# First projection of two dense MLP layers as seven block products, with pairs of column chunks and a joined ReLU and square

## The reference, cut to what matters

```python
def sq_relu_mlp(h, w1, w2):
    return jnp.square(jax.nn.relu(h @ w1)) @ w2
# h: 256 tokens x 1024,  w1: 1024 x 4096,  w2: 4096 x 1024   (twice: after S5, after attention)
```

## Time and profile before

| | |
|---|---|
| median of three timed runs | 1896.58 us |
| the profiled execution | 1891.4 us |
| its span, first to last instruction | 1889.4 us |
| TensorE busy | 1585.1 us, 84% |
| VectorE busy | 635.8 us, 34% |
| ScalarE busy | 231.5 us, 12% |
| mean granted TensorE clock | 0.924 |

### The profile page before, as it was taken

How to read it: one execution, slowest core, us unless ns; L and a number is a source line. 1 busy time by engine, 2 the same in 40 slices (tenths; PEclk the granted TensorE clock), 3 DMA queues, 4 the chain that set the end, 5 groups by cost and what they waited for, 6 DMA issues and landing times. The chain is left out here.

```text
span 1889.4 us, 28141 instructions
## 1 busy us (share of the span) xinstructions
PE 1585.1 (84%) x12561; PEld 1011.5 (54%) x12561; DVE 635.8 (34%) x1409; ACT 231.5 (12%) x519; POOL 75.3 (4%) x95
## 2 busy tenths in 40 slices
PE   8999768778776999966575756699999999999998
PEld 6654434444433885533232323488688446578743
DVE  5752233432233224212411111360213463421356
ACT  2311011001100000200200000120011002311000
POOL 2000100000000100000000000060000001000000
PEclk9999889888988999987888878799999999999999
DMA  9457999999998846899999999933534444234420
GB/s 334 151 225 285 383 425 425 425 425 423 424 425 347 322 185 279 348 420 424 412 407 426 421 426 422 382 147 132 192 140 152 153 138 159 90 134 148 164 89 22
DMA packets 88070, 540.03 MB, mean 286 GB/s; under 512 B 7342, under 2 KB 9454, under 8 KB 54156
## 3 DMA queue, kind: packets, MB, share of 16 engines
q1 hardware_dynamic: 86060, 531.24, 70.1%
q0 software_dynamic: 1888, 6.95, 1.0%
HBM read 531.89 MB, written 6.29 MB: 285 GB/s over the span
## 5 line engine op out<-in xcount | busy, mean ns | idle before, releaser
L759 PE MATMUL ps<-ring,work 128*32 128x256 f32 x3968 | 296.7, 460 | 224.4 <-DMA ring<-in_moe_w_up 222.7
L759 PEld LDWEIGHTS ps<-ring,work 128*32 128x32 f32 x3968 | 156.3, 127 | 352.6 <-issue 297.1
L710 PE MATMUL ps<-hT,ring 128*128 128x256 f32 (+2 forms) x1424 | 312.6, 382 | 0.0
L710 PEld LDWEIGHTS ps<-hT,ring 128*128 128x128 f32 x1424 | 269.8, 190 | 41.9 <-issue 2.5
L2115 DVE TENSOR_TENSOR rowb<-rowb,ps 128x128 f32<-128x128 f32 x64 | 18.3, 287 | 383.0 <-ACT rowb L1544 383.0
L772 PE MATMUL ps<-ring,multi 128*32 128x256 f32 x1984 | 122.5, 388 | 12.5 <-ACT multi L1549 12.5
L2121 DVE COPY multi<-ps 128x256 f32<-128x256 f32 x64 | 27.1, 424 | 264.4 <-PE ps L772 264.4
L1251 PE MATMUL ps<-ring,work 128*128 128x512 f32 x256 | 114.4, 592 | 0.0
L736 PE MATMUL ps<-ring,work 128*128 128x512 f32 x256 | 110.9, 593 | 0.0
L772 PEld LDWEIGHTS ps<-ring,multi 128*32 128x32 f32 x1984 | 58.9, 111 | 74.4 <-issue 23.7
L1251 PE MATMUL ps<-work 128*128 128x512 f32 x192 | 87.0, 592 | 0.0
(11 more groups left out here) (481 smaller groups left out, 1562.1 us busy)
## 6 DMA issues: line engine op xcount, KB each, us to landing
ring<-in_moe_w_gate SPq DMA_DIRECT2D x62, 2048.0 KB, 18.8
ring<-in_moe_w_up SPq DMA_DIRECT2D x62, 2048.0 KB, 23.4
ring<-in_moe_w_down SPq DMA_DIRECT2D x62, 2048.0 KB, 22.5
ring<-in_w_ff SPq DMA_DIRECT2D x32, 2048.0 KB, 8.3
ring<-in_sc_w_in SPq DMA_DIRECT2D x6, 2048.0 KB, 17.9
ring<-in_ssm_w_glu SPq DMA_DIRECT2D x4, 2048.0 KB, 19.1
ring<-in_lru_w_in SPq DMA_DIRECT2D x3, 2048.0 KB, 14.2
ring<-in_lru_w_out SPq DMA_DIRECT2D x2, 2048.0 KB, 23.5
```

The costliest lines, as they stand in the source:

```text
L710: mm = pe.matmul(ps[:, bank, 0:n], w[:, k, P * c:P * c + P], hT[:, k, t0:t0 + n], start=(k == 0), stop=(k == DC - 1))
L759: mm = pe.matmul(ps[32 * q:32 * q + 32, bank, 0:256].rearrange("p (u n) -> p u n", u=2), x[:, k, :], gu[:, k, :, 2 * P * (q // 2):2 * P * ...
```

## The change

Tokens and contraction are cut in two, and so are the two column chunks of a pair: with A the tokens (two blocks of 128 by two halves of the contraction of 512) and B the weights (two halves by two chunks of 128), seven products of sums of blocks replace eight products of blocks. A product is four accumulating matmuls of 128x128 by 128. VectorE makes three sums of weight blocks and one in place for each piece of w1 (`first_weights`), four sums of token blocks once a layer (`first_tokens`), and joins the seven products of each pair (`join`) after ScalarE copied one of them out of PSUM. The last instruction of the join takes the ReLU and the square in one. A pair takes two PSUM banks, and four pairs are in flight. The weight sums of pieces 0 and 1 are made before `mix_norm`. The attention's `oT` moves to another region.

```diff
-        for kind in ("ff_proj", "ff_relu", "ff_sq"):
-            share(kind, [(f"{kind}{l}", DFF // P) for l in range(2)])
+        for kind in ("ff_pair", "ff_copied", "ff_sq"):
+            share(kind, [(f"{kind}{l}", NPAIR) for l in range(2)])
...
-                add(f"ff1_{layer}_{j}", cols(a["w_ff1_2"][layer], 512 * j, 512), (f"ff_proj{layer}", 4 * j + 4))
+                add(f"ff1_{layer}_{j}", cols(a["w_ff1_2"][layer], 512 * j, 512), (f"ff_pair{layer}", 2 * j + 2))
...
+        pair_bank = ((2, 6), (3, 7), (4, 0), (5, 1))
+        def pair_part(j, first, n=1):
+            bank, at = next((pair_bank[j % 4][i], row.index(first)) for i, row in enumerate(((2, 6, 1, 3), (4, 5, 7))) if first in row)
+            return ps[:, bank, P * at:P * at + P * n]
...
+        def first_factors(layer, j, i):
+            p_, q = j // 2, j % 2
+            t1, t2, t4 = (t[:, :, q, :] for t in first_sums(p_))
+            b11, t3, b21, b22 = (piece_of(layer, p_, k1, e)[:, :, q, :] for k1 in range(2) for e in range(2))
+            return {1: (b11, hT_b[0][:, 0:4]), 2: (b21, hT_b[0][:, 4:8]), 3: (b22, ff_s4), 4: (t4, hT_b[1][:, 4:8]),
+                    5: (t1, ff_s1), 6: (t2, ff_s2), 7: (t3, ff_s3)}[i]
...
-        oT = region(7424, HEADS, SEQ)
+        oT = region(8192, HEADS, SEQ)
...
+            def pair_product(layer, j, i):
+                w, x = first_factors(layer, j, i)
+                for k in range(4):
+                    mm = pe.matmul(pair_part(j, i), w[:, k, :], x[:, k, :], start=(k == 0), stop=(k == 3), skip_group_check=True)
+                return mm
             def ff_first(layer, before_):
+                transposes(before_, [1, 2], f"{before_}_normed", only=0)
+                pe.wait_ge(*nth(f"{before_}_hT", 2))
+                for j in range(4):
+                    slot_wait(pe, f"ff1_{layer}_{j // 2}")
+                    for i in (1, 2):
+                        pair_product(layer, j, i)
+                transposes(before_, [1, 2], f"{before_}_normed", only=1)
+                pe.wait_ge(*nth(f"{before_}_hT", 4))
+                for j in range(4):
+                    pe.wait_ge(*nth(f"ff_weights{layer}", j // 2 + 1))
+                    pair_product(layer, j, 4)
+                pe.wait_ge(*nth(f"ff_tokens{layer}", 1))
+                for j in range(4):
+                    for i in (6, 5, 7, 3):
+                        mm = pair_product(layer, j, i)
+                    mm.then_inc(S(f"ff_pair{layer}"), 1)
+                for j in range(4, NPAIR):
+                    slot_wait(pe, f"ff1_{layer}_{j // 2}")
+                    pe.wait_ge(*nth(f"ff_sq{layer}", j - 3))
+                    for i in (1, 2):
+                        pair_product(layer, j, i)
+                    pe.wait_ge(*nth(f"ff_weights{layer}", j // 2 + 1))
+                    for i in (6, 5, 7, 4, 3):
+                        mm = pair_product(layer, j, i)
+                    mm.then_inc(S(f"ff_pair{layer}"), 1)
...
-                    pe.wait_ge(*nth(f"ff_sq{layer}", 4 * j + 4))
+                    pe.wait_ge(*nth(f"ff_sq{layer}", NPAIR - 1 if j == 0 else NPAIR))
...
-                    A(ff[:, c, :], ps[:, ff_bank(c), 0:SEQ], ACT.Relu).then_inc(S(f"ff_relu{layer}"), 1)
+                for j in range(NPAIR):
+                    act.wait_ge(*nth(f"ff_pair{layer}", j + 1))
+                    if j >= 4:
+                        act.wait_ge(*nth(f"ff_sq{layer}", j - 3))
+                    A(ff_p1[j % 4], pair_part(j, 1), ACT.Copy).then_inc(S(f"ff_copied{layer}"), 1)
...
+            def first_weights(layer, p_):
+                b11, b12, b21, b22 = (piece_of(layer, p_, k1, e) for k1 in range(2) for e in range(2))
+                t1, t2, t4 = first_sums(p_)
+                slot_wait(dve, f"ff1_{layer}_{p_}")
+                if p_ >= 4:
+                    dve.wait_ge(*nth(f"ff_pair{layer}", 2 * p_ - 2))
+                link(V.tensor_tensor(t1, b12, b11, ALU.subtract))
+                V.tensor_tensor(b12, b22, b12, ALU.subtract)
+                link(V.tensor_tensor(t2, b22, t1, ALU.subtract))
+                V.tensor_tensor(t4, b21, t2, ALU.subtract).then_inc(S(f"ff_weights{layer}"), 1)
+            def first_tokens(layer, before_):
+                a11, a12, a22 = hT_b[0][:, 0:4], hT_b[0][:, 4:8], hT_b[1][:, 4:8]
+                dve.wait_ge(*nth(f"{before_}_hT", 4))
+                link(V.tensor_tensor(ff_s1, ff_s3, a22, ALU.add))
+                V.tensor_tensor(ff_s3, a11, ff_s3, ALU.subtract)
+                link(V.tensor_tensor(ff_s2, ff_s1, a11, ALU.subtract))
+                V.tensor_tensor(ff_s4, a12, ff_s2, ALU.subtract).then_inc(S(f"ff_tokens{layer}"), 1)
+            def join(layer, j):
+                two_ = lambda t: t.rearrange("p (a n) -> p a n", a=2)
+                one = lambda t: t.unsqueeze(1).to_broadcast([P, 2, P])
+                even, odd, u = ff[:, 2 * j, :], ff[:, 2 * j + 1, :], two_(ff_u)
+                dve.wait_ge(*nth(f"ff_copied{layer}", j + 1))
+                link(V.tensor_tensor(two_(even), one(ff_p1[j % 4]), two_(pair_part(j, 2, 2)), ALU.add))
+                link(V.tensor_tensor(u, one(even[:, P:2 * P]), two_(pair_part(j, 5, 2)), ALU.add))
+                V.tensor_tensor(odd[:, 0:P], u[:, 0], pair_part(j, 3), ALU.add)
+                link(V.tensor_tensor(ff[:, 2 * j:2 * j + 2, P:2 * P], one(u[:, 1]), two_(pair_part(j, 4, 2)), ALU.add))
+                both = ff[:, 2 * j:2 * j + 2, :]
+                V.scalar_tensor_tensor(out=both, in0=both, scalar=0.0, in1=both, op0=ALU.max, op1=ALU.mult).then_inc(S(f"ff_sq{layer}"), 1)
+            def mlp(layer, before_):
+                first_tokens(layer, before_)
+                first_weights(layer, 2)
+                for j in range(NPAIR):
+                    join(layer, j)
+                    if j == 1:
+                        first_weights(layer, 3)
+                    elif j % 2 and 5 <= j < 12:
+                        first_weights(layer, (j + 3) // 2)
+                    elif j in (13, 15):
+                        piece_sums(layer, (j - 13) // 2)
...
+            for p_ in range(2):
+                first_weights(0, p_)
             mix_norm("s5")
...
+            for p_ in range(2):
+                first_weights(1, p_)
             mix_norm("mla")
```

More of the change, by code:

```diff
@@ L62 @@
 DFF = 4 * D
+NPAIR = DFF // P // 2
 BIG = 1.0e30
@@ L115, in first_and_second_block @@
         share("masked", [(f"masked{l}", 3 - l) for l in range(2)])
-        for kind in ("ff_proj", "ff_relu", "ff_sq"):
-            share(kind, [(f"{kind}{l}", DFF // P) for l in range(2)])
+        for kind in ("ff_pair", "ff_copied", "ff_sq"):
+            share(kind, [(f"{kind}{l}", NPAIR) for l in range(2)])
+        share("ff_weights", [(f"ff_weights{l}", 8) for l in range(2)])
+        share("ff_tokens", [(f"ff_tokens{l}", 1) for l in range(2)])
         share("dve_constants", [("par_ready", 1), ("lam", 1), ("soft", 1), ("p_half", 1), ("p_theta", 1), ("s5_coef", 1),
@@ L316, in region, with piece_of, first_sums @@
             return v
-        def ff_bank(c):
-            return 2 + c % 4 if c < DFF // P - 4 else (1, 6, 7, 5)[c % 4]
+        pair_bank = ((2, 6), (3, 7), (4, 0), (5, 1))
+        def pair_part(j, first, n=1):
+            bank, at = next((pair_bank[j % 4][i], row.index(first)) for i, row in enumerate(((2, 6, 1, 3), (4, 5, 7))) if first in row)
+            return ps[:, bank, P * at:P * at + P * n]
+        def piece_of(layer, p_, k1, e):
+            w = slot_view(f"ff1_{layer}_{p_}", DC, 512).rearrange("p k (q e n) -> p k q e n", q=2, e=2)
+            return w[:, 4 * k1:4 * k1 + 4, :, e, :]
+        def first_sums(p_):
+            at = (2048, 5120)[p_] if p_ < 2 else 8192 + 4096 * (p_ % 2)
+            return [region(at + 1024 * i, 4, 2, P) for i in range(3)]
+        hT_b = [hT[:, :, NMETA + P * b:NMETA + P * b + P] for b in range(2)]
+        ff_s1, ff_s2, ff_s4 = (t.rearrange("p (k n) -> p k n", k=4) for t in (rowb[:, 0:512], rowb[:, 512:1024], tmp_a[:, 0:512]))
+        ff_s3 = hT_b[1][:, 0:4]
+        ff_p1 = [tmp_a[:, 512 + P * i:512 + P * i + P] for i in range(4)]
+        ff_u = multi[:, 2048:2048 + 2 * P]
+        def first_factors(layer, j, i):
[4 more added lines that the diff above has]
+                    5: (t1, ff_s1), 6: (t2, ff_s2), 7: (t3, ff_s3)}[i]
         product_bank = {1: 2, 2: 0, 3: 1, 4: 7, 5: 4, 6: 3, 7: 6}
@@ L1233, in _ @@
             rows_out("s5", [1, 2], ["s5_out0", "s5_out1"], s5_y, NMETA, "glu_done")
-            def ff_first(layer, before_):
[L1237 to L1245, removed]
+            def pair_product(layer, j, i):
[3 more added lines that the diff above has]
+                return mm
+            def ff_first(layer, before_):
+                transposes(before_, [1, 2], f"{before_}_normed", only=0)
[23 more added lines that the diff above has]
+                    mm.then_inc(S(f"ff_pair{layer}"), 1)
             def product(layer, i, j):
@@ L1266, in ff_second @@
```

(20 more changed lines are left out.)

## The result

The changed kernel took 1870.26 us (median of four runs, 1868.70 to 1873.58) against 1894.44 us before (four runs, 1890.48 to 1896.86): ratio 0.9875, 95% interval 0.9858 to 0.9892. The forecast was 1873 us in a range of 1865 to 1884. The profiled execution took 1868.7 us, with a span of 1866.9; the sum had given 1869.6.

What follows compares the result with a forecast made beforehand. TensorE's matmul instruction count times spacing was taken to bound both first projections; saving 21.8 us from 1891.4 gave 1869.6 by the profiled execution, 1874.8 on the median's scale. Forecast 1873 us, range 1865 to 1884.

Steps and rivals of the forecast that it cites:

- The distance of matmuls: First projections: matmul instructions 128 columns wide follow each other every 0.1117 us, 256 wide every 0.2158; upper bound 0.1153.
- TensorE, term by term: First projections, after the second token block is ready: 103.85 us becomes 92.93 for 832 instructions, saving 10.9 us a layer.
- VectorE's new work: Beside the first projections: join 2.3 us, weight sums 4.9, token sums 2.8; VectorE keeps up with 3 us to spare.
- The due times: When TensorE wants each VectorE result in the first projections: no stall booked, up to 1 us a layer allowed.
- The hand-over: Start of the second projection: join 14 waits behind w2's 6.13 us piece sums, ready 91.5, wanted 92.9, cover 1.4 us.
- Due time (1): Token sums at the first projection's start: ready 2.8 us, wanted 3.57; at contended speed 4.1, 0.5 us late.
- Ahead of the norm: Before the MLP norm: the first two weight sums, 9.8 us, fit VectorE's idle 12.90 and 13.31 us.
- Sum: Whole kernel: 1891.4 less 21.8 gives 1869.6 us by the profiled execution, 1874.8 on the median's scale; 1873 given.
- A: First projections: contended VectorE becomes the bound, join 3.45 us; with undisturbed sums from about 4.4; 1907 us, chance 0.05.
- B: Only the hand-over stalls: joins of 3.5 to 4.0 us make join 14 late; 1875 to 1884 us, chance 0.09.
- C: First projections: each 128-wide instruction waits for its own 192 ns weight load; 2004 us, chance 0.01.
- D: First projections: spacing is 0.1153 us and each group end costs 0.03 us; gain 12 us, 1885 us, chance 0.05.

Runs made afterwards that it cites:

- e1: Kernel before, with its first projections' eight products done 128 columns wide instead of 256; 1902.39 us, ratio 1.0043.
- e3: Changed kernel with two dummy linked 512-element VectorE sums at the head of each join; 1874.54 us, ratio 0.9898.
- e4: Changed kernel with three dummy linked 512-element VectorE sums at the head of each join; 1898.38 us, ratio 1.0016.
- e6_pool_later: Changed kernel with GpSimd's broadcasts of the MLP norm's gains held back until the token sums are made; 1872.46 us, ratio 0.9885.

## Why the prediction was right

1. *The distance of matmuls.* Right. 0.1117 was read from ReLUs 16 instructions apart and came out at 0.1118 in the changed kernel and 0.11175 in e1. The run's own quotient, 7.38 / 64 = 0.1153, would have given 7.9 us a layer: it carries the last matmul's passage through the array.
2. *TensorE, term by term.* 92.93 us forecast for the 832 instructions; 93.01 and 93.38 measured. Saved 10.90 and 10.53 a layer against 10.9. The 72 more group ends and the waits between them cost nothing visible: 800 instructions in one unbroken piece of the chain. The second MLP's 0.37 us more than the first's is the token sums' wait, with the slower start of the product behind it.
3. *VectorE's new work.* Join 2.24 us (2.3), weight sums 4.8 (4.9), the joined ReLU and square 0.692 (0.70). The stretch was 73% busy, a little under the 75 to 80 named.
4. *The due times.* The hand-over's cover was 1.45 us (1.4), and e3 confirmed it by using it up. Due time (1) came true in the worse of its two forms, for the second MLP: GpSimd's contention made the sums 3.9 us long (4.1 in the bound) and TensorE 0.3 us late (0.5). I had booked up to 1 us a layer for this and the hand-over.
5. *Ahead of the norm.* Right: the idle time left ahead of line 1813 shrank from 12.90 and 13.31 us to 3.31 and 3.73, and the stretch of line 768 is as long as before, 27.47 us.
6. *Sum.* 21.8 us forecast, 21.7 in the changed stages. The median was a guess between 1869.6 and 1874.8: the 5.2 us by which the three runs before lay above the profiled one didn't carry over. A fourth run brought the median before to 1894.44. That 1873 came within 3 us of the median owes something to luck. The medians differ by 24.2 us, 2.5 more than the stages account for; the interval (0.9858 to 0.9892, 20 to 27 us) holds both.
7. *Rivals.* A's mechanism didn't occur: the join's instructions ran at the undisturbed rows' speed, 2.24 us and not 3.45, and GpSimd rests in those stretches (0.00 us after as before), as I had argued. What such a length would cost was sized about right: e4 made the join 2.24 + 3 x 0.73 = 4.43 us long, where A said it decides, and its ratio is 1.0016. A's sum had no term for the clock, about 2 us a layer in e4. B needed a join of 3.5 us; e3's 3.7 cost 1.4 us a layer by the gap, by the due times 1.5. C and D's spacing are refuted by e1, and D's price of a group end by the changed kernel's own 0.1118.

The rule of the Trainium skill that a load overlaps matmuls only of other row groups ("TensorE: Matmul & The Clock Gate", The mechanism) does not hold in these runs: e1 has 960 full 128x128 loads beside 960 matmuls at 0.11175 us. The same section also lets a load into the background weight buffer go ahead of running matmuls, which would allow what is seen here, though no row tells one such load from another; the prediction quoted only the stricter half. On the token sums the Trainium skill is right: "SBUF — State Buffer", Who interferes with whom, says that a VectorE instruction with two SBUF inputs contends with a GpSimd instruction that reads SBUF. The rows agree, 1.02 and 1.53 us beside the broadcast and 0.69 without it. Whether a VectorE instruction with one input in PSUM is spared, these runs don't show, since the joins were never beside GpSimd.

## What to carry to other kernels

Where one engine is busy without a gap, price a change by its count of instructions times the spacing for their exact shape, read from events a known number of instructions apart, and never from the duration column. Then write the other engine's due times as a list and look for the one with the least cover: here it was not the steady loop with 3 us to spare in 12.5, but the end of it, where another stage's sums stand in line before the last two joins. Work added under such cover costs next to nothing until the knee and then nearly all of itself: 23 us of VectorE work a layer cost 1.5, the next 12 cost about another 11. Some 2 of those 11 us are TensorE's clock at 1.2 GHz behind its 8 us wait, so a long wait costs more than its own length.

## What the runs showed of the hardware that was not expected

A GpSimd broadcast slows VectorE's SBUF-to-SBUF sums more than the 1.04 us of the earlier trace rows, and is itself slowed: a 512-element sum went from 0.69 to as much as 1.69 us (e3_join_plus2), and a pair of broadcasts from 2.45 to as much as 4.22 us (e6_pool_later). Which of the sums is hit changes from run to run with no change in the kernel: in the changed kernel it was above all the second one in the second MLP, 1.53 us, and in its repeat the first one alone, 1.68 us, with the pair of broadcasts at its plain 2.45.

TensorE's granted clock fell from 1.00 to 0.50 while it waited 8.27 us for a join (e4_join_plus3), and its first instructions behind the wait cost about 2 us more than at full clock. The gaps of 0.74 and 1.44 us left it at 1.00.
